# A two-layer encoder trunk on one core: the opening stage rearranged (x in eight slices, first weights in halves, two queues, products in order of arrival)

## The reference

```
h = x * rsqrt(mean(x*x, -1) + eps) * norm_mix_g[0]
b, c, xt = split(h @ conv_w_in, 3)        # 1024 x 3072
z = c * xt;  conv = causal depthwise conv of width 3 over tokens
x = x + (b * conv) @ conv_w_out
```

## Time and profile before

| what | value |
|---|---|
| time, median of 3 runs | 1103.15 us (1100.79 to 1103.56) |
| the profiled execution's own time | 1103.38 us |
| its span | 1101.4 us |
| busy TensorE / VectorE / ScalarE / GpSimd | 1079.7 / 828.4 / 472.2 / 189.6 us |
| first turn of x starts | 5.69 us |
| first useful product starts | 9.84 us |
| column sums start | 25.00 us |
| second block of the first projection starts | 34.17 us |
| mean granted clock of TensorE | 0.996 |

### The profile page before, as it was taken

One profiled execution on the slowest core, in us unless ns is written; L12 is line 12 of the kernel. 1 busy time (PEld: TensorE's weight loads), 2 busy tenths in 40 slices (PEclk: granted clock), 3 DMA queues, 4 the chain that ended last, 5 costly groups with the idle time before them and its releaser, 6 DMA issues.

```text
span 1101.4 us, 18699 instructions
## 1 busy us (share of the span) xinstructions
PE 1079.7 (98%) x6732; PEld 961.1 (87%) x6732; DVE 828.4 (75%) x1181; ACT 472.2 (43%) x698; POOL 189.6 (17%) x145
## 2 busy tenths in 40 slices
PE   8999999999999999999999998989999999999997
PEld 7888888999999997888888755779999999978887
DVE  5655659999999998434457899499999999984443
ACT  6222236544345455222355466365444454552122
POOL 6000001322332220111200000013323332201010
PEclk9999999999999999999999999999999999999999
DMA  6333242233233333333332002022333233333321
GB/s 196 95 96 108 82 115 77 78 115 114 86 105 114 114 91 104 96 105 112 100 96 70 8 20 58 1 77 78 114 114 98 93 114 114 98 100 91 105 65 77
DMA packets 144039, 101.68 MB, mean 92 GB/s; under 512 B 3912, under 2 KB 142336, under 8 KB 144000
## 3 DMA queue, kind: packets, MB, share of 16 engines
q1 hardware_dynamic: 143648, 100.61, 30.3%
q0 software_dynamic: 320, 0.55, 0.2%
q10 hardware_dynamic: 32, 0.01, 0.0%
HBM read 99.06 MB, written 2.10 MB: 92 GB/s over the span
## 4 chain that ended last, share of the span: by engine, by line
PE 69%; DVE 6%; ACT 3%; issue 2%; DVEq 0%; ACTq 0%
PE ps L375 22%; PE ps L377 22%; PE ps L376 22%; DVE prob L1322 1%; ACT prob L900 1%; ACT hid_hi L763 1%; DVE wgt_lo L359 1%; PE ps L1620 1%; DVE prob L1338 1%; DVE x_op_lo L1068 0%; PE ps L436 0%; PE ps L1683 0%; PE ps L1699 0%; ACT x_op_hi L727 0%; DVE prob_T L1348 0%
## 5 line engine op out<-in xcount | busy, mean ns | idle before, releaser
L375 PE MATMUL ps<-x_op_hi,op_w_hi 128*128 128x256 f32 x1232 | 350.0, 284 | 2.9 <-DVE x_op_lo L1068 2.8
L376 PE MATMUL ps<-x_op_lo,op_w_hi 128*128 128x256 f32 x1232 | 349.3, 284 | 0.0
L377 PE MATMUL ps<-x_op_hi,op_w_lo 128*128 128x256 f32 x1232 | 349.3, 284 | 0.0
L375 PEld LDWEIGHTS ps<-x_op_hi,op_w_hi 128*128 128x128 f32 x1232 | 237.2, 192 | 3.5 <-DVE x_op_lo L1068 3.0
L376 PEld LDWEIGHTS ps<-x_op_lo,op_w_hi 128*128 128x128 f32 x1232 | 237.3, 193 | 0.1
L377 PEld LDWEIGHTS ps<-x_op_hi,op_w_lo 128*128 128x128 f32 x1232 | 237.2, 193 | 0.0
L375 PE MATMUL ps<-hid_hi,wgt_hi 128*128 128x512 f32 (+1 forms) x550 | 211.5, 384 | 2.1 <-DVE hid_lo L1125 2.1
L377 PE MATMUL ps<-hid_hi,wgt_lo 128*128 128x512 f32 (+1 forms) x550 | 209.5, 381 | 0.0
L376 PE MATMUL ps<-hid_lo,wgt_hi 128*128 128x512 f32 (+1 forms) x550 | 209.4, 381 | 0.0
L359 DVE TENSOR_TENSOR wgt_lo<-raw,wgt_hi 128x1024 fp32r<-128x1024 f32 (+4 forms) x131 | 138.4, 1073 | 91.0 <-ACT wgt_hi L350 89.7
L641 POOL TENSOR_TENSOR w_sum<-pair_raw 128x512 f32<-128x512 f32 x44 | 59.6, 1356 | 645.5 <-DMA pair_raw<-in_ffn_w_gate 341.3
(11 more groups left out here) (167 smaller groups left out, 1221.9 us busy)
## 6 DMA issues: line engine op xcount, KB each, us to landing
pair_raw<-in_ffn_w_gate SPq DMA_DIRECT2D x22, 1024.0 KB, 5.4
pair_raw<-in_ffn_w_up SPq DMA_DIRECT2D x22, 1024.0 KB, 5.4
raw<-in_conv_w_in SPq DMA_DIRECT2D x24, 512.0 KB, 3.8
raw<-in_ffn_w_down SPq DMA_DIRECT2D x32, 384.0 KB, 3.6
raw<-in_ffn_w_down SPq DMA_DIRECT2D x32, 320.0 KB, 2.9
raw<-in_conv_w_out SPq DMA_DIRECT2D x8, 512.0 KB, 3.7
raw<-in_mla_w_o SPq DMA_DIRECT2D x8, 512.0 KB, 3.9
x_nat<-in_x SPq DMA_DIRECT2D x4, 512.0 KB, 7.0
```

What stands on the lines that cost most here:

```text
L375: nc.tensor.matmul(acc, wh, xh, start=first, stop=False)
L376: nc.tensor.matmul(acc, wh, xl, start=False, stop=False)
L377: return nc.tensor.matmul(acc, wl, xh, start=False, stop=last)
```

## The change

`x` comes in eight slices of 128 features, each with a semaphore of its own. The first two slices are issued by ScalarE, slice 0 ahead of the gain rows of the mixer norms and slice 1 behind them; the others by SP. The first three weight units come in halves (four chunks each): three first halves early in SP's order, the rests between slices of `x`. ScalarE and VectorE split each half by itself. TensorE turns a chunk and multiplies in an order written out by hand, over all three units. GpSimd squares chunk 0 straight into `sq_sum`, with no clearing and no addition. The column sums are issued one block of tokens at a time with a product behind each. The core of the diff:

```diff
+        HALF_W = DC // 2 * P
+        def load_x(eng, m):
+            eng.dma_start(x_nat[:, :, m * P:(m + 1) * P],
+                          x_dram.rearrange("(t p) d -> p t d", p=P)[:, :, m * P:(m + 1) * P]).then_inc(x_in[m], 16)
+        def load_front(eng, u):
+            src, n, width = source("conv_in", 0, u)
+            dst = raw[:, u, 0:HALF_W].rearrange("p (c n) -> p c n", n=width)
+            eng.dma_start(dst, src[:, 0:n // 2, :]).then_inc(front_in[u], 16)
...
         @block.sync
             sp.dma_start(ident, consts[:, 0:P]).then_inc(ident_in, 16)
-            load_x(0)
-            load_unit(sp, "conv_in", 0, 0)
-            load_x(1)
-            load_unit(sp, "conv_in", 0, 1)
-            load_x(2)
-            load_x(3)
+            load_front(sp, 0)
+            load_front(sp, 1)
+            load_x(sp, 2)
+            load_front(sp, 2)
+            load_x(sp, 3)
+            load_rest(sp, 0)
+            load_x(sp, 4)
+            load_rest(sp, 1)
+            load_x(sp, 5)
+            load_rest(sp, 2)
+            load_x(sp, 6)
+            load_x(sp, 7)
...
-            clear_sum(0)
-            for m in range(X_POOL):
+            pool.wait_ge(x_copied, 1)
+            nc.gpsimd.tensor_tensor(sq_sum[:, :], xT[:, 0, :], xT[:, 0, :], ALU.mult).then_inc(sq_added, 1)
+            for m in range(1, X_POOL):
                 add_square(0, m, x_copied, m + 1)
...
         @block.scalar
+            load_x(sc, 0)
             sc.dma_start(gain_rows[0:2 * DC, :],
                          w["norm_mix_g"].rearrange("l (r c) -> (l r) c", c=P)).then_inc(mix_in, 16)
+            load_x(sc, 1)
...
+            x_hi_of(0)
+            front_hi_of(0)
+            x_hi_of(1)
+            front_hi_of(1)
+            x_copy(0)
+            x_hi_of(2)
+            front_hi_of(2)
+            x_copy(1)
+            x_hi_of(3)
+            x_copy(2)
+            rest_hi_of(0)
+            x_hi_of(4)
+            x_copy(3)
+            rest_hi_of(1)
+            x_hi_of(5)
+            x_copy(4)
+            rest_hi_of(2)
+            x_hi_of(6)
+            x_copy(5)
+            x_hi_of(7)
+            x_copy(6)
+            x_copy(7)
...
         @block.vector
+            x_lo_of(0)
+            front_lo_of(0)
+            x_lo_of(1)
+            front_lo_of(1)
+            x_lo_of(2)
+            front_lo_of(2)
+            x_lo_of(3)
+            rest_lo_of(0)
...
         @block.tensor
+            def first_product(u, k):
+                if k == 0:
+                    pe.wait_ge(front_lo, u + 1)
+                if k == DC // 2:
+                    pe.wait_ge(w_lo, u + 1)
+                pe.wait_ge(x_lo, k + 1)
...
+            turn_x(0)
+            keep_warm(3)
+            turn_x(1)
+            first_product(0, 0)
+            first_product(0, 1)
             turn_x(2)
+            first_product(1, 0)
+            first_product(1, 1)
             turn_x(3)
+            first_product(0, 2)
+            first_product(1, 2)
+            first_product(2, 0)
+            first_product(2, 1)
             turn_x(4)
+            first_product(0, 3)
+            first_product(1, 3)
             turn_x(5)
+            first_product(2, 2)
+            first_product(0, 4)
             turn_x(6)
+            first_product(2, 3)
+            first_product(1, 4)
+            first_product(0, 5)
             turn_x(7)
+            first_product(1, 5)
+            first_product(0, 6)
             pe.wait_ge(gain_in, 16 * 5)
             pe.wait_ge(gain_ready, 1)
             turn_gains(G_ROWS)
+            first_product(2, 4)
+            first_product(0, 7)
             pe.wait_ge(gain_ready, 2)
             pe.wait_ge(sq_added, X_POOL)
             pe.wait_ge(sq_rest, 2)
             pe.wait_ge(x_copied, DC)
-            column_sums([sq_sum, c_r])
-            chunk_products("conv_in", 0, 2, every[1:5], x_lo, 0)
+            for t, (u, k) in enumerate(((1, 6), (1, 7), (2, 5))):
+                column_sum([sq_sum, c_r], t)
+                first_product(u, k)
+            column_sum([sq_sum, c_r], TB - 1).then_inc(stat_done, 1)
+            first_product(2, 6)
             make_rows(pe, 0)
-            chunk_products("conv_in", 0, 2, every[5:], x_lo, 0)
+            first_product(2, 7)
             later_bodies("conv_in", x_lo, 0)
```

More of the change, by code:

```diff
@@ L232, in trunk_kernel @@
         ident_in, tables_in, mix_in, gain_in = sem("ident_in"), sem("tables_in"), sem("mix_in"), sem("gain_in")
-        x_in = [sem(f"x_in{c}") for c in range(4)]
+        x_in = [sem(f"x_in{c}") for c in range(8)]
+        front_in = [sem(f"front_in{u}") for u in range(3)]
+        front_hi, front_lo = sem("front_hi"), sem("front_lo")
         raw_in = [sem(f"raw_in{s}") for s in range(4)]
@@ L429, in trunk_kernel, with column_sum @@
         ROOT = {0: 0, 1: 1, 2: 2, 3: 5, 4: 6}
-        SQ_NEW = [X_POOL, X_POOL + 2 * DC - 1]
+        SQ_NEW = [X_POOL - 1, X_POOL + 2 * DC - 2]
+        def column_sum(parts, t):
+            for n, part in enumerate(parts):
+                ins = nc.tensor.matmul(ps[:, STAT_BANK, t:t + 1], part[:, t * P:(t + 1) * P], ones[:, 0:1],
+                                       start=n == 0, stop=n == len(parts) - 1)
+            return ins
         def column_sums(parts):
             for t in range(TB):
-                for n, part in enumerate(parts):
-                    ins = nc.tensor.matmul(ps[:, STAT_BANK, t:t + 1], part[:, t * P:(t + 1) * P], ones[:, 0:1],
-                                           start=n == 0, stop=n == len(parts) - 1)
+                ins = column_sum(parts, t)
             ins.then_inc(stat_done, 1)
@@ L572, in _ @@
                 ub, n = shape[name][0:2]
-                for u in range(2 if name == "conv_in" else 0, ub):
+                for u in range(3 if name == "conv_in" else 0, ub):
                     if name.startswith("down") and u % 2 == 0 and u < 4:
@@ L617, in clear_sum @@
             def clear_sum(n):
[L618 to L619 removed]
+                pool.wait_ge(stat_done, ROOT[n])
                 nc.gpsimd.memset(sq_sum[:, :], 0.0).then_inc(sq_zero, 1)
@@ L627, in add_square @@
                                         xT[:, ds(m, 1), :].rearrange("p a s -> p (a s)"), ALU.mult).then_inc(sq_new, 1)
-                wait(pool, sq_new, m + (squares_before(n) + 1 - n // 2))
-                pool.wait_ge(sq_zero, n // 2 + 1)
+                wait(pool, sq_new, m + (squares_before(n) - n // 2))
+                if n:
+                    pool.wait_ge(sq_zero, n // 2)
                 nc.gpsimd.tensor_tensor(sq_sum[:, :], sq_sum[:, :], sq[:, :], ALU.add).then_inc(sq_added, 1)
@@ L691, in _, with x_hi_of, x_copy, front_hi_of @@
             sc.wait_ge(gain_ready, 1)
[L692 to L702, removed]
+            def x_hi_of(m):
+                sc.wait_ge(x_turned, m + 1)
+                nc.scalar.activation(xg_hi[:, m, :], ps[:, X_BANK + m % X_BANKS, :], ACT.Copy,
+                                     scale=gain[:, rows["mix0"] + m:rows["mix0"] + m + 1]).then_inc(x_hi, 1)
+            def x_copy(m):
+                sc.wait_ge(x_lo, m + 1)
+                nc.scalar.activation(xT[:, m, :], ps[:, X_BANK + m % X_BANKS, :], ACT.Copy).then_inc(x_copied, 1)
+            def front_hi_of(u):
+                sc.wait_ge(front_in[u], 16)
+                nc.scalar.activation(wgt_hi[:, u, 0:HALF_W], raw[:, u, 0:HALF_W], ACT.Copy).then_inc(front_hi, 1)
+            def rest_hi_of(u):
+                sc.wait_ge(raw_in[u], 16)
+                nc.scalar.activation(wgt_hi[:, u, HALF_W:1024], raw[:, u, HALF_W:1024], ACT.Copy).then_inc(w_hi, 1)
+            x_hi_of(0)
[20 more added lines that the diff above has]
+            x_copy(7)
             sc.wait_ge(x_copied, DC)
@@ L981, in gain_lo, with x_lo_of @@
                                                chunk(xg_hi, m).bitcast(F32), ALU.mult, ALU.subtract).then_inc(x_lo, 1)
-            for m in range(DC):
+            def x_lo_of(m):
                 ve.wait_ge(x_hi, m + 1)
@@ L987, in _, with front_lo_of, rest_lo_of @@
                                                xg_hi[:, m, :].bitcast(F32), ALU.mult, ALU.subtract).then_inc(x_lo, 1)
-                if m in (0, 3, 6):
-                    unit_lo(ve, *plan["home"][m // 3])
+            def front_lo_of(u):
+                ve.wait_ge(front_hi, u + 1)
+                nc.vector.tensor_tensor(wgt_lo[:, u, 0:HALF_W], raw[:, u, 0:HALF_W], wgt_hi[:, u, 0:HALF_W].bitcast(F32),
+                                        ALU.subtract).then_inc(front_lo, 1)
+            def rest_lo_of(u):
+                ve.wait_ge(w_hi, u + 1)
+                nc.vector.tensor_tensor(wgt_lo[:, u, HALF_W:1024], raw[:, u, HALF_W:1024],
+                                        wgt_hi[:, u, HALF_W:1024].bitcast(F32), ALU.subtract).then_inc(w_lo, 1)
+            x_lo_of(0)
[6 more added lines that the diff above has]
+            rest_lo_of(0)
+            x_lo_of(4)
+            rest_lo_of(1)
+            x_lo_of(5)
```

(38 more changed lines are left out.)

9 lines of the change are left out of this document (4 added, 5 removed).

## The result

The changed kernel takes 1110.38 us (median of 4 runs, 1109.44 to 1112.4) against 1103.35 (4 runs): ratio 1.0072, interval 1.0051 to 1.0092. It is 7 us slower; forecast were 1105.0 and a range to 1107.5. The profiled execution took 1109.44 us with a span of 1107.7, which is 6.3 us over the span before. A granted clock is stated for each execution's span: 0.996 before, 0.993 in this one, 0.992, 0.992 and 0.989 in the other three, so the profiled one is the fastest of the four.

The account below looks back on a forecast made before the run. The start of the second block was taken as the bound: 28.3 + 1.8 + 3.85 + 0.81 + 0.1 + 1.1 = 35.95 us against 34.17; 1.7 us later after a rounding allowance, so 1105 us, range 1101 to 1107.5.

Parts of the forecast that it names:

- The gain rows behind slice 0: Opening, ScalarE's queue: gains arrive between 3.4 and 5.2 us, taken as 4.4; first turn at 6.45, 0.75 us later.
- the late last turn: TensorE's opening: 15 products and five turns put the last turn of x at 22.4 us instead of 17.80.
- the wait ahead of the sums: TensorE before the column sums: idles 2.6 us where it idled 0.3, sums starting at 28.3 us.
- the wait for the bank at the second block: TensorE at the second block's start: waits 1.1 us for VectorE's reading of bank 0, one product covering instead of three.
- the stepping: ScalarE and VectorE followed in their new order: each low part ready at least 0.1 us ahead of its product.
- a sign that the prediction fails: Opening: a product waiting for a half unit was listed as one of three observations that would refute the prediction.
- that the clock stays up: Condition on the second block starting 1.8 us later: TensorE's clock does not fall; the old 1.6 us loss is saved.
- Sums to second block: Column sums 1.8 us, five products 3.85, rows 0.81, root and reciprocal 0.1, wait for the bank 1.1.
- a rival with half the weight of the forecast: Around the column sums: the clock falls again after the longer idleness, +1.6 us at most, 1106.6 us; chance 0.23.
- both clock rivals: Clock rising late in the opening and falling again near the column sums: 1108 us together; chances 0.08 and 0.23 singly.
- the clock rises late: Opening: a gap of about 1 us delays full clock past 9.85, up to 1.6 us lost, 1106.6 us; chance 0.08.
- Worth nothing by itself: GpSimd's dropped addition (1.3 us) and clearing (0.5 us): gain nothing alone, only shortening what ran beside VectorE's adds.

Follow-up runs that it names:

- the wait filled: Changed kernel with nine unused 512-column matmuls on TensorE in its wait ahead of the column sums; ratio 1.0048 to the kernel before.
- the sums together: Changed kernel with its column sums issued together again and the three products behind them; ratio 1.0060 to the kernel before.
- the kernel with slices: Kernel before with x in eight slices on two queues, weight units whole, engine order untouched; ratio 1.0021 to the kernel before.

## Why the prediction was wrong

**Direction and places were right.** The gain rows behind slice 0, the late last turn, the wait ahead of the sums, the wait for the bank at the second block and the hidden arrival of x were all forecast, each at its place: no product waits for x. Two low parts were late, which the stepping had at least 0.1 us early: that of the first half unit by 0.2 us and that of chunk 1 by 0.2. The first was named as a sign that the prediction fails; it only says that the first product comes when its chain is done, and that was 3.38 us behind the turn, 3.4 forecast.

**The term that failed is the proviso "that the clock stays up".** Sums to second block were put at 7.66 us (1.8 + 3.85 + 0.81 + 0.1 + 1.1) and took 10.35. With the wait filled the same stretch takes 7.38: the sum was 0.3 us too long, and the clock is 3.0 us of what it took. It was set up as a rival with half the weight of the forecast, though the same profile showed the clock falling behind 0.3 us of idleness, and I was adding 2.3 us to this. The better reading: the forecast's own wait was the rival's condition.

**Its bound was wrong too.** "+1.6 at most" took the one stretch of before as the price. The clock was low for twice as long (6.8 against 3.4 us), 3.4 us short, of which the smaller wait for the bank gives some back (0.8 us, where it is 1.0 with the wait filled). A fall was worth 2.7 us more than the sum, which alone makes 1107.6. The range was short by its own terms too: both clock rivals on top of 1104.9 are 1108.1, which the range to 1107.5 was said to take in.

**The start.** Gains at 4.95, not 4.4: 0.55 us, inside the bounds given (3.4 to 5.2), near the upper one, as two queues that share would have it. From the first product to the last turn 13.39 us instead of 12.55, 0.84 more. With the sums together, where the code up to there is the same and the first matmuls ran at the full clock, it took 12.83. So 0.3 us were missing from the sum, and about 0.6 come from a clock that rose late: slow first steps, and a second turn at half speed (1.06 us against 0.60) with `xg_lo` of chunk 1 late behind it. That is the rival "the clock rises late" in a small form. Whether the turns themselves help to raise the clock no run separates: every kernel has warm matmuls among them. The chain from the last turn to the sums took 5.70 us, 5.9 forecast.

The sum: the first product 0.53 late, then 0.84 - 0.20 + 2.69, together 3.86, which is 39.82 less 35.96 (the prediction's terms add up to this, not to 35.95). Another 0.65 us of the span arises behind the second block and is not traced to an instruction. The three executions without a trace took 0.9 to 3.0 us more than the profiled one; their mean clocks (0.992, 0.992, 0.989 against 0.993) are lower, so they spent more time at the lower level, in a part of the span that no trace shows.

**The unsummed square was underrated.** "Worth nothing by itself" holds in the changed kernel, where the last turn is late. In the kernel before it frees VectorE's second add and brings the sums forward by about 0.5 us (from the turn: 6.74 against 7.20), which also takes away the wait ahead of them.

## What to carry to other kernels

A wait that a change adds on TensorE is priced with the clock, not by its own length: 2.2 us of waiting brought 3.0 us of lower clock with it here, and filling it with useless matmuls gave these back. Where a kernel's own executions differ by the clock, as those of the kernel before do by 4 us, compare many executions before one trace is believed. Before an opening is reordered by arrival, follow the last item, not the first: what everything behind depends on (here the last turn of x) must not be pushed behind products that could wait. And a small transfer that the first instruction needs goes ahead of a large one in its queue.

## What the runs showed of the hardware

The clock's fall follows the wait loosely. The traces of the three kernels with a wait of 2.2 us ahead of the sums each show 6.8 us at the lower level, beginning 0.4 to 2.2 us behind the wait; one execution in fourteen of these kernels seems to have escaped it. A wait of 0.3 us ahead of sums that stand together had 3.4 us at the lower level in the kernel before. With products between the sums and the same wait there were none in three kernels, and without the wait none in two, but the kernel before has executions with as high a mean clock, so these five traces alone don't show what kept it up. Waits of 1.7 and 1.9 us for x, at 7 to 9 us, had none in the two kernels with the unsummed square, while 1.2 and 1.8 us in the kernel with slices had 6.8. One trace each.

In the first microseconds of a trace the granted clock reads 1.00 while the steps show less: the warm matmuls of the kernel before stand 0.26 us apart ahead of 5.7 us and 0.14 at 6.85, and the column reads 1.00 in every microsecond from 2 to 8.

Two loaded queues side by side gave the smaller transfer no advantage: 256 KB issued at about 1.2 us let TensorE start at 6.63 (beside whole units) and at 5.86 to 6.00 (beside half units, three kernels), where 512 KB issued at 1.20 at the head of a single queue let it start at 5.16 to 5.69 in four.

VectorE's add of 128 by 512 with both inputs in SBUF takes 0.69 us alone and 1.15 to 1.66 us beside GpSimd's additions, as the adds of these kernels show.
